# Cross attention's head norms: VectorE adds the two tiles of squares of a head, and the token sums move in between the scores of two halves

## The reference, cut to what matters

```
def memory_cross_attention(hn, memn, wq, wkv, q_norm_g, k_norm_g, wo):
    q = rms_norm((hn @ wq).reshape(B, S, XATTN_HEADS, XATTN_HEAD_DIM), q_norm_g)
    k, v = jnp.split(memn @ wkv, 2, axis=-1)
    k = rms_norm(k.reshape(B, M, XATTN_HEADS, XATTN_HEAD_DIM), k_norm_g)
    v = v.reshape(B, M, XATTN_HEADS, XATTN_HEAD_DIM)
    s = jnp.einsum('bshd,bmhd->bhsm', q, k) / math.sqrt(XATTN_HEAD_DIM)
    p = jax.nn.softmax(s, axis=-1)
    return jnp.einsum('bhsm,bmhd->bshd', p, v).reshape(B, S, D_MODEL) @ wo
```

## Time and profile before

| | us |
|---|---|
| median of 3 runs | 2159.54 (2159.36 to 2159.71) |
| the profiled execution, its own time | 2159.2 |
| its span in the profile | 2157.4 |
| TensorE busy (matmul) | 2142.9, 99% of the span |
| TensorE weight loads busy | 1758.8, 82% |
| VectorE busy | 1143.5, 53% |
| ScalarE busy | 905.0, 42% |

### The profile page before, as it was taken

The page is one execution under the profiler, slowest core; times in us unless marked ns, Lnnn a source line. Parts: engine busy times, 40 slices in busy tenths (PEclk is TensorE's granted clock), DMA queues, the critical chain, the costliest instruction groups (busy, mean ns, idle before and its releaser), DMA issues.

```text
span 2157.4 us, 29375 instructions
## 1 busy us (share of the span) xinstructions
PE 2142.9 (99%) x12086; PEld 1758.8 (82%) x12086; DVE 1143.5 (53%) x1965; ACT 905.0 (42%) x1530; POOL 0.2 (0%) x4
## 2 busy tenths in 40 slices
PE   9999999999999999999999999999999999999999
PEld 7888988888888888888888878877667888888887
DVE  4665664453433454344357677747775455434345
ACT  6655445442322332222234466546766233212224
POOL 0000000000000000000000000000000000000000
PEclk9999999999999999999999999999999999999999
DMA  5121621133333333323223622321111323233321
GB/s 188 59 79 60 211 82 59 59 98 98 98 98 98 98 98 97 99 90 104 86 91 91 204 82 84 98 84 50 45 31 40 98 98 98 98 98 98 98 88 69
DMA packets 190199, 199.54 MB, mean 92 GB/s; under 512 B 7777, under 2 KB 185074, under 8 KB 189554
## 3 DMA queue, kind: packets, MB, share of 16 engines
q1 hardware_dynamic: 190066, 197.66, 29.0%
HBM read 188.73 MB, written 2.10 MB: 88 GB/s over the span
## 4 chain that ended last, share of the span: by engine, by line
PE 96%; DVE 1%; ACT 1%; issue 1%; DMA 0%; SPq 0%; DVEq 0%; ACTq 0%
PE lin L557 28%; PE lin L559 27%; PE lin L558 27%; PE turned L658 3%; PE score L755 3%; PE mix L769 2%; PE mix L1219 1%; PE score L1038 1%; PE mix L1058 1%; PE score L871 1%; PE score L1022 0%; PE mix L779 0%; DMA raw<-in_w_in_dram 0%; PE mix L1285 0%; ACT arena L1487 0%
## 5 line engine op out<-in xcount | busy, mean ns | idle before, releaser
L557 PE MATMUL lin<-xh,wh 128*128 128x512 f32 (+1 forms) x1478 | 582.1, 394 | 1.8 <-DVE wl L2147 1.2
L559 PE MATMUL lin<-xh,wl 128*128 128x512 f32 (+1 forms) x1478 | 569.3, 385 | 0.0
L558 PE MATMUL lin<-xl,wh 128*128 128x512 f32 (+1 forms) x1478 | 568.3, 385 | 0.0
L557 PE MATMUL lin<-ah,wh 128*128 128x512 f32 x1044 | 408.5, 391 | 0.2 <-DVE h L2200 0.2
L559 PE MATMUL lin<-ah,wl 128*128 128x512 f32 x1044 | 406.1, 389 | 0.0
L558 PE MATMUL lin<-al,wh 128*128 128x512 f32 x1044 | 406.0, 389 | 0.0
L2141 DVE TENSOR_TENSOR wl<-raw,wh 128x2048 fp32r<-128x2048 f32 x129 | 295.7, 2293 | 185.4 <-ACT wh L1389 185.4
L1389 ACT ACTIVATE wh<-raw 128x2048 fp32r<-128x2048 f32 x129 | 245.8, 1906 | 263.6 <-PE lin L559 263.6
L557 PEld LDWEIGHTS lin<-xh,wh 128*128 128x128 f32 x1478 | 278.2, 188 | 63.5 <-issue 10.3
L559 PEld LDWEIGHTS lin<-xh,wl 128*128 128x128 f32 x1478 | 277.9, 188 | 56.1
L558 PEld LDWEIGHTS lin<-xl,wh 128*128 128x128 f32 x1478 | 278.5, 188 | 52.2 <-issue 1.0
(11 more groups left out here) (350 smaller groups left out, 2088.0 us busy)
## 6 DMA issues: line engine op xcount, KB each, us to landing
raw<-in_ffn_w_dram SPq DMA_DIRECT2D x60, 1024.0 KB, 5.3
raw<-in_w_in_dram SPq DMA_DIRECT2D x38, 1024.0 KB, 5.2
raw<-in_mlp_w_dram SPq DMA_DIRECT2D x32, 1024.0 KB, 5.3
raw<-in_xattn_wkv_dram SPq DMA_DIRECT2D x8, 1024.0 KB, 5.4
raw<-in_w_out_dram SPq DMA_DIRECT2D x8, 1024.0 KB, 5.1
arena<-arena SPq DMA_DIRECT2D x104, 64.0 KB, 2.0
raw<-in_ffn_w_dram SPq DMA_DIRECT2D x8, 768.0 KB, 4.6
raw<-in_xattn_wq_dram SPq DMA_DIRECT2D x4, 1024.0 KB, 5.2
```

The source lines that it names most:

```text
L557: nc.tensor.matmul(o, w[0], x[0], start=first, stop=False)
L558: nc.tensor.matmul(o, w[0], x[1], start=False, stop=False)
L559: return nc.tensor.matmul(o, w[1], x[0], start=False, stop=last)
```

## The change

VectorE gets a new step, `both_squares(j, n)`: it waits for both tiles of squares and adds tile 1 to tile 0 in place, counting `xn_ad`. TensorE's `pair_sums` and `token_sums` wait for that count, where they waited for ScalarE's squares, and make the sums from `C_sq[:, 0]` alone, with half as many matmuls. `token_sums` writes to `ps[1]`, and is placed between the scores of the two token tiles of a head's first group; VectorE reads the sums between the two maxima. For the keys `both_squares(k // 2, M)` stands at the head of VectorE's loop for even k; for the queries it stands at the head of the step in which a head's first group starts.

```
@@ -267,6 +267,7 @@
+        xn_ad = sem("xn_ad")
@@ -982,12 +983,10 @@
             def pair_sums(j, n):
 
-                pe.wait_ge(xn_sq, 2 * j + 2)
+                pe.wait_ge(xn_ad, j + 1)
                 if j >= 2:
                     pe.wait_ge(xn_std, j - 1)
-                for c in range(2):
-                    mm = nc.tensor.matmul(po[j % 2][:, 0:n], ones, C_sq[:, c, 0:n], start=c == 0, stop=c == 1)
-                mm.then_inc(xn_mm, 1)
+                nc.tensor.matmul(po[j % 2][:, 0:n], ones, C_sq[:, 0, 0:n], start=True, stop=True).then_inc(xn_mm, 1)
@@ -1016,10 +1015,9 @@
                 def token_sums(hd):
-                    pe.wait_ge(xn_sq, 8 + 2 * hd + 2)
+                    pe.wait_ge(xn_ad, 4 + hd + 1)
                     for t in range(QT):
-                        for c in range(2):
-                            mm = nc.tensor.matmul(ps[0][:, M + t:M + t + 1], C_sq[:, c, t * PART:(t + 1) * PART], ones[:, 0:1], start=c == 0, stop=c == 1)
+                        mm = nc.tensor.matmul(ps[1][:, M + t:M + t + 1], C_sq[:, 0, t * PART:(t + 1) * PART], ones[:, 0:1], start=True, stop=True)
                     mm.then_inc(xn_mm, 1)
@@ -1029,11 +1027,12 @@
                     if u == 0:
-                        token_sums(hd)
                         for c in range(2):
                             pe.wait_ge(lin_freed[c], P0["xq"] + hd + 1)
                     for a in range(2):
                         tok = slice((2 * u + a) * PART, (2 * u + a + 1) * PART)
+                        if u == 0 and a == 1:
+                            token_sums(hd)
                         for e in range(2):
@@ -2533,6 +2532,11 @@
+            def both_squares(j, n):
+
+                dve.wait_ge(xn_sq, 2 * j + 2)
+                nc.vector.tensor_tensor(C_sq[:, 0, 0:n], C_sq[:, 0, 0:n], C_sq[:, 1, 0:n], ALU.add).then_inc(xn_ad, 1)
+
             def head_norm(j, buf, gain, n):
@@ -2549,6 +2553,8 @@
             for k in range(KT):
+                if k % 2 == 0:
+                    both_squares(k // 2, M)
                 dve.wait_ge(ld_h[k // 4], 16)
                 add(P0["wout"] + k // 2, k % 2, h[:, k, :], 1.0)
@@ -2585,15 +2591,14 @@
                 def most(g):
                     hd, u = g // 2, g % 2
-                    dve.wait_ge(at_s[0], U + g + 1)
-                    if u == 0:
-                        if hd:
-                            dve.wait_ge(xq_v, 3 * hd)
-                        dve.wait_ge(xq_r, 2)
-                        nc.vector.tensor_tensor(C_ms, ps[0][:, M:M + QT], C_r2, ALU.mult).then_inc(xq_ms, 1)
                     for a in range(2):
                         at = g % 2 * 4 + a
                         dve.wait_ge(at_s[a], U + g + 1)
+                        if u == 0 and a == 1:
+                            if hd:
+                                dve.wait_ge(xq_v, 3 * hd)
+                            dve.wait_ge(xq_r, 2)
+                            nc.vector.tensor_tensor(C_ms, ps[1][:, M:M + QT], C_r2, ALU.mult).then_inc(xq_ms, 1)
                         dve.wait_ge(at_p[a], U + g)
@@ -2623,6 +2628,8 @@
                 for s in range(XA_STEP[-1] + 4):
+                    if s in group and group[s] % 2 == 0:
+                        both_squares(4 + group[s] // 2, T)
                     if s - 3 in group:
                         g = group[s - 3]
```

## The result

The changed kernel takes 2175.83 us (median of 5 runs, 2175.3 to 2176.8), the kernel before, run beside it, 2159.36 (2159.24 to 2159.71). The ratio is 1.0076, with a 95% interval of 1.0066 to 1.0087: 16.5 us slower. The forecast was 2169.1 with a range up to 2175.0. The sign was right, the size was not, and the time lies just above the range.

A forecast was written before the change was run, and what follows sets the result against it. TensorE was taken to bound the kernel; -1.72 + 0.1 + 11.85 + 1.9 - 2.52 = +9.6 us on the profiled 2159.2 gave 2168.8, or 2169.1 as median. The range was 2166.5 to 2175.0 us.

The forecast's parts named there:

- What bounds the kernel: TensorE's matmuls cover 99% of the span; time taken from its queue comes off, time it stands comes on top.
- What is removed: Half of TensorE's pair_sums (1.72 us) and token_sums (3.36 us) instructions go, together 5.1 us.
- The stalls of pair_sums 1 to 3: Keys: TensorE waits for VectorE's addition, queued behind conversion and head_norm; 3.95 us each, undiminished, 11.85 us in all.
- Head 0: First token sums in the attention: TensorE stands from 324.45 to 327.0 for VectorE's addition; net cost 1.9 us.
- Heads 1 to 3: Token sums of the later attention heads: additions in time, each head saves its whole 0.84 us, -2.52 us together.
- the sum: Savings, stalls and head costs together make the kernel 9.6 us slower; bounds 2167.2 to 2170.7 us.
- The clock: At pair_sums, stalls of about 3.7 us end just short of a fall at 3.9; head 0's 2.6 should be harmless.
- Rival 1: The clock falls in some of the stalls: two falls of three at 2.7 us each, 2174.5 us; 20% chance.
- Rivals 2 and 3: VectorE's additions hidden everywhere, 2154.4 us, 4%; additions in the attention push VectorE's own work onto the path, 2171.2 us, 7%.

The follow-up runs named there:

- e8: e7 with the keys' head_norm(j) put a panel later, ahead of VectorE's conversion where it was idle: 2154.91 us against 2159.55 for the kernel before.
- e5: e4 with the token sums ahead of both tiles of scores again: 2156.86 us against 2159.72 for the kernel before.
- e3: The changed kernel plus unused TensorE matmuls ahead of pair_sums 1 to 3 and the first token sums: 2169.18 us, ratio 1.0045 to the kernel before.
- e1: The changed kernel with the keys' half undone, so only the queries get the addition: 2160.23 us against 2159.48 for the kernel before.
- e2: The changed kernel with the queries' half undone, so only the keys get the addition: 2174.07 us, ratio 1.0068 to the kernel before.
- e4: e1 with head 0's addition ahead of VectorE's conversion of the third query panel: 2155.94 us against 2159.48 for the kernel before.
- e7: e4's queries, plus the keys' change with squares and additions ahead of ScalarE's copy and VectorE's conversion: 2158.76 us against 2159.72 for the kernel before.
- e6: e4's queries, plus the keys' change with the addition between VectorE's conversion and head_norm: 2159.34 us against 2159.72 for the kernel before.

## Why the prediction was wrong, by its own steps

**What bounds the kernel**: right. Every part of the stalls came on top.

**What is removed.** Right. pair_sums flow in 0.43 us (0.86 before) where nothing stalls them, token_sums in 0.79 (1.68 before; 0.84 was forecast). With both hidden, e8 shows 4.6 of the 5.1 us.

**The stalls of pair_sums 1 to 3.** Right in cause and size. The addition took 0.42 us, as interpolated, and started right behind head_norm. The rest of TensorE was 3.8 us and the refilling 0.2, against 3.95 in all; it came back whole each time (3.83, 3.79, 3.79).

**Head 0**: the stall was right (2.55 us against 327.0 - 324.45 = 2.55). **Heads 1 to 3**: right, no wait; e5 shows that the place between the scores is what hides the one at head 3 (0.5 us, forecast 0.6). Together these make the +9.6 of the sum, and e3, with the clock held, measures +9.7. (The lower bound of that sum was added up a little wrong: its terms give 2167.0, not 2167.2. Nothing hangs on it.)

**The clock.** This is the step that failed: it put the clock's cost at nothing. I read from the end of the trace that the clock fell 3.9 us after the last matmul and took that for the rest that TensorE must have before it falls, so that 3.7 us end "just short of a fall", and for head 0 I read 2.56 us of rest at the start of the trace as harmless. The change showed a fall behind all three long stalls, and behind the one of 2.6 as well, in e1 too; in none of these during the rest, always after work had begun again. In e2 two came during the rest, after 3.2 and 3.7 us of it. One case at the end, with nothing running behind it, and one at the start, where TensorE had not been working before, didn't have the situation that was asked about: a rest between two stretches of work. The trace of before held no such case of more than 1.2 us, and the honest bound would have been a fall behind each of the four stalls. The 3.9 us were not even a fixed quantity: at the end of e4's trace the clock falls 2.6 us after the last matmul (2148.7 to 2151.3), at the end of e7's 5.3 us after it (2149.65 to 2154.9). The rule of the Trainium skill ("TensorE: Matmul & The Clock Gate", section "HAM oscillation — how this bites in real kernels"), that gaps in its work that are long enough throttle TensorE again each time, was the better guide. By the change's trace it holds, four gaps and four falls of some 1.6 us; e6 shows the other side, a gap of 1.2 us with the clock at 1.00. The "each time" isn't borne out by e2, where one gap of 3.8 us of three had no fall behind it.

Rival 1 had the mechanism with 20%, two falls of three at 2.7 us each, 2174.5. Measured were four falls at 1.6 us, 6.6 us in all (6.65 by e3). Its price per fall was too high, its number of falls too low; by luck the two errors nearly cancel. With the price that was measured, four falls give 2169.1 + 4 x 1.6 = 2175.5. That some falls come should have been the likeliest case; the price and the number could not have been read from the trace of before.

**Rivals 2 and 3**: no sign of either. The stalls of the keys were not hidden, and the additions at heads 1 to 3 pushed nothing onto the path.

## What to carry to other kernels

Work that is taken from the bounding engine and given to one with time to spare must be in time, not only small: look up where in the other engine's queue it comes to stand and what is ahead of it; here 0.42 us of addition stood behind 2.6 us of a norm that nobody needed yet, and put earlier it brought a gain. An engine at 53% can be nearly level with the bounding one in a single stage (0.35 us of 11.79 to spare), so count its loop there, waits included, before giving it more (e7 against e8). And a stall of TensorE in the middle of dense work is priced at its length and, from 2.6 us on here, at a possible fall of the clock: 1.6 us in six cases of eight, nothing in one and 2.9 in one. The end of a trace, where nothing runs any more, says nothing of that price.

## What the runs showed of the hardware that I had not expected

The granted clock fell to 0.50 at rests of 3.8 and 2.6 us (seven falls in eight such rests, in the change, e1 and e2) and stayed at 1.00 through those of 1.2 us in e6 and of 1.8 in e7. Five of the seven falls came when TensorE was at work again, up to 1.6 us after its restart, the two of e2 while it stood, one of them 0.1 us before the restart. In the change seven or eight dense matmuls of 512 columns then took 0.43 us each until it rose (0.23 at full clock), in e2 once twelve, with TensorE at work all the time. Useless matmuls into a free bank while waiting held it at 1.00 and made the kernel 6.65 us faster than resting did.

e1's ten runs lie in two groups, six at 2159.9 to 2160.3 us with a mean clock of 0.999 and four at 2161.4 to 2161.8 with 0.998, 1.5 us apart. The profile is of the first group, so the cause isn't known; a fall of twice the length, as e2 has one, would fit as well as a second fall.
